# Scan of a hybrid RWKV-7 / Conformer encoder: feature loads on ScalarE's queue, lower blocks and diagonals ahead of the keys at the begin

## The chip, the cores and the metric

The kernel runs on one core of one Trainium2 chip. The metric is the device time of one execution in microseconds; the median of three executions of the kernel before is 2488.1 us (2484.7 to 2490.22).

## The reference

Two groups of tokens (512 and 1024) pass through one encoder layer. What matters here is the RWKV-7 branch: for every head (8 heads of width 64) and for both directions a state is carried over the tokens, and the outputs of the two directions are summed.

```python
def wkv7_scan(r, logw, k, v, a, b, reverse):
    # S_t = S_{t-1} diag(exp(-exp(logw_t))) + (S_{t-1} a_t) b_t^T + v_t k_t^T ;  y_t = S_t r_t
    def step(S, inp):
        r_t, w_t, k_t, v_t, a_t, b_t = inp
        sa = jnp.einsum('bhij,bhj->bhi', S, a_t)
        S = (S * w_t[:, :, None, :] + sa[..., :, None] * b_t[..., None, :]
             + v_t[..., :, None] * k_t[..., None, :])
        return S, jnp.einsum('bhij,bhj->bhi', S, r_t)
    ...
```

Ahead of it lie a norm and one projection into 38 column tiles; after it come a Conformer convolution branch, the merge of the branches, an output projection and a layer of 16 experts of which each takes its best tokens.

## The kernel before, in words

The program has three stages one after the other: `project` and `scan` in one block, then `mixing`, then `experts`. The change lies in the scan and in one helper that `project` uses as well.

**The scan** cuts the 1536 tokens into 24 chunks of 64 (`NCH`), numbered i = 0 to 23 in the order in which a direction d takes them. Within a chunk the recurrence is turned into matrix work: products of the features of a chunk with each other (`products`, `products_c`, lines 376 to 410), masked on VectorE (`masked`, `masked_c`, L412 to L433), a triangular inverse, and then the step itself: `solve` (L1502), `full` (L1516), `state` (L1528). The products run `AHEAD` = 4 chunks ahead of the step. `body(i)` (L1548) is the order of TensorE in step i: `level_n` (L1472) of chunk i, `solve` of chunk i - 1, `level_x` (L1485, L1489), `full(0)` of chunk i - 1, products of chunk i + 4, and so on. `body_first` (L1573) is its order at the begin: the levels of chunk 0, and the products of chunks 2, 3 and 4. L384, L387, L392 and L395 are lines of `products`, and L408 is that of `products_c`.

**Features.** The factors that `products` multiplies are written to HBM by `project` and read back in pairs of chunks. `features(sp, m)` (L345) issues two loads of 1 MB, one for each direction, into one of two buffers (m % 2), after waiting until the products and the receptance copies of pair m - 2 are done. `project` issues m = 0 and 1; the scan issues m = 2 to 11, all of them on SyncE's queue (L1386, L1398, L1433), m = 2 and 3 at the begin and the others in steps 2, 4, ..., 16.

**The triangular inverse.** The lower block of a chunk goes from SBUF to HBM (`lower`, L355, four issues for a chunk), and its 16x16 diagonal blocks come back in another layout (`diagonal`, L363, two issues). For a pair of chunks GpSimd inverts the diagonal blocks (`invert`, L1717), SyncE stores them (`inverses`, L1361) and loads them in the layout of the step (`compact`, L1371), GpSimd spreads them (`expand`, L1739, whose instruction is L1745), and TensorE's `level_n` reads the result.

**SyncE's queue** holds all loads of the scan in an order that is written out by hand (L1383 to L1450): per step also `tokens` (L1330, four issues), `keys` (L1343) and `values` (L1352), two issues each. A wait holds all that stands behind it.

**ScalarE** (L1679 to L1709) in step i: two `gh` copies (`solved`, what `full` reads), the `xx` copies of the levels, the receptance copies of chunk i + 4, and the output copies with their stores to HBM. After step 9 it also computes an inverse root (`conv_root`, L1656), after steps 12 and 13 `conv_silu`.

**VectorE** at the begin (L1913 to L1933): `masked` and `masked_c` of chunks 2, 3 and 4 with the levels of chunk 0 among them, and `started()` (L1788), which writes the decay factors, a state of zeros and identities that step 1 is the first to read. It stands between the work on chunk 3 and that on chunk 4:

```python
            for d in DIRS:
                e.masked_c(dve, d, 3, EARLY)
            started()
            e.masked(dve, 0, AHEAD, EARLY)
            e.masked(dve, 1, AHEAD, EARLY)
```

## Time and profile before

| | |
|---|---|
| median of three executions | 2488.1 us (2484.7 to 2490.22) |
| profiled execution | 2486.42 us, its span 2484.6 us |
| TensorE busy | 2329.5 us (94%) |
| VectorE busy | 1823.7 us (73%) |
| ScalarE busy | 1211.8 us (49%) |
| GpSimd busy | 722.4 us (29%) |
| mean granted TensorE clock | 0.975 |
| SyncE's DMA queue | 412.52 MB in 275552 packets |
| ScalarE's DMA queue | 37.82 MB in 11296 packets |
| queue of instructions (q8) | 1.95 MB in 119 packets |
| feature loads | 24 issues of 1 MB, median 6.1 us from issue to landing |

The span runs from the first to the last instruction of the profiled execution; its own time is 1.8 us longer. Busy time of TensorE is that of matmuls, whose ends are modelled, so a TensorE that is busy is not one at its peak. The scan takes the stretch from about 760 to 1160 us, the projection what lies ahead of it. In the rows, PE is TensorE's matmul, PEld its weight load, DVE VectorE, ACT ScalarE, POOL GpSimd, SPq SyncE's queue; "[3.31 <-DVE all L422]" means that the engine was idle for 3.31 us before the row and that VectorE's instruction of line 422 released it, and "<-issue" that nothing which the profile shows held it.

### The profile page before, as it was taken

How to read it: one execution, taken by the hardware profiler on the slowest of the kernel's cores; microseconds unless marked ns; L12 is line 12 of the kernel's file. 1: busy time of each engine (PE TensorE's matmuls, PEld its weight loads, DVE VectorE, ACT ScalarE, POOL GpSimd, SP SyncE). 2: the span in 40 equal slices, each digit the busy share in tenths (PEclk: the TensorE clock that was granted, in tenths of full speed). 3: DMA queues.
4: the chain of work that ended last, by engine and by line, in shares of the span. 5: the costliest groups of instructions: out<-in, count | busy, mean ns of one | idle time of the engine just before them, and what ended most of it. 6: DMA issues, size and time to landing. Idle time of an engine off the chain costs nothing. (4 is left out here: it accounts for less than half of the span.)

```text
span 2484.6 us, 50105 instructions
## 1 busy us (share of the span) xinstructions
PE 2329.5 (94%) x19520; PEld 2034.6 (82%) x19520; DVE 1823.7 (73%) x2475; ACT 1211.8 (49%) x1751; POOL 722.4 (29%) x721
## 2 busy tenths in 40 slices
PE   6899999999998999987999995799999999999997
PEld 3688888888887999985766674799999999999996
DVE  4547888988895676674767677677777777777777
ACT  5355444544522334433334332665656666666556
POOL 2233243442422444464454535011111111101111
PEclk9999999999998999998999997899999999999998
DMA  4325243352566766763647352877777777777777
GB/s 153 86 88 163 92 158 115 114 174 73 169 206 187 208 190 192 194 169 109 222 128 253 111 198 99 322 256 260 261 246 239 251 259 254 246 252 266 261 254 245
DMA packets 294772, 479.74 MB, mean 193 GB/s; under 512 B 142224, under 2 KB 209952, under 8 KB 266832
## 3 DMA queue, kind: packets, MB, share of 16 engines
q1 hardware_dynamic: 275552, 412.52, 50.5%
q0 software_dynamic: 7760, 27.08, 4.9%
q10 hardware_dynamic: 11296, 37.82, 4.7%
q8 instruction: 119, 1.95, 0.3%
q14 instruction: 45, 0.37, 0.0%
HBM read 363.51 MB, written 110.69 MB: 191 GB/s over the span
## 5 line engine op out<-in xcount | busy, mean ns | idle before, releaser
L2975 PE MATMUL bank<-e_xt,e_w_high 128*128 128x384 f32 x1792 | 525.3, 357 | 3.5 <-DVE e_xt L3143 2.2
L3130 DVE TENSOR_TENSOR e_w_low<-e_w,e_w_high 128x2048 fp32r<-128x2048 f32 x192 | 436.4, 2286 | 69.3 <-ACT e_w_high L3031 69.3
L2976 PE MATMUL bank<-e_xt,e_w_low 128*128 128x192 f32 x1792 | 449.3, 251 | 0.0
L3031 ACT ACTIVATE e_w_high<-e_w 128x2048 fp32r<-128x2048 f32 x192 | 366.5, 1909 | 108.0 <-PE bank L2997 79.3
L2976 PEld LDWEIGHTS bank<-e_xt,e_w_low 128*128 128x128 f32 x1792 | 342.5, 191 | 0.6
L2975 PEld LDWEIGHTS bank<-e_xt,e_w_high 128*128 128x128 f32 x1792 | 338.2, 189 | 5.3 <-issue 2.5
L712 PE MATMUL bank<-h_high,w_high 128*128 128x512 f32 x864 | 259.3, 408 | 1.2 <-DVE work L1158 1.2
L1141 DVE SCALAR_TENSOR_TENSOR work<-work,vec 128x1551 f32<-128x1551 f32 x116 | 243.2, 2096 | 2.2
L715 PE MATMUL bank<-h_low,w_high 128*128 128x512 f32 x864 | 244.2, 391 | 0.0
L718 PE MATMUL bank<-h_high,w_low 128*128 128x512 f32 x864 | 243.5, 390 | 0.0
L2909 POOL DMA_INDIRECT xacc_dram<-e_y,e_put x30 | 47.3, 1577 | 648.3 <-DVE e_y L3165 643.8
L838 POOL TENSOR_TENSOR w_low<-w,w_high 128x1024 fp32r<-128x1024 f32 x38 | 100.4, 2641 | 317.0 <-ACT w_high L887 317.0
L715 PEld LDWEIGHTS bank<-h_low,w_high 128*128 128x128 f32 x864 | 162.6, 188 | 35.6
L718 PEld LDWEIGHTS bank<-h_high,w_low 128*128 128x128 f32 x864 | 162.2, 188 | 34.8
L712 PEld LDWEIGHTS bank<-h_high,w_high 128*128 128x128 f32 x864 | 155.1, 189 | 34.1 <-issue 8.2
L3223 DVE TENSOR_TENSOR e_sums<-bank,e_sums 128x192 f32<-128x192 f32 x256 | 79.2, 350 | 140.1 <-ACT e_sums L3076 140.1
L2144 POOL TENSOR_TENSOR x_w_low<-x_w,x_w_high 128x1024 fp32r<-128x1024 f32 x48 | 118.7, 2473 | 143.2 <-ACT x_w_high L2409 143.1
L3076 ACT ACTIVATE e_sums<-bank 128x192 f32<-128x192 f32 x256 | 70.7, 328 | 150.4 <-PE bank L2979 150.3
L1622 ACT ACTIVATE xx<-bank 128x512 f32<-128x512 f32 (+1 forms) x96 | 46.8, 492 | 171.4 <-PE bank L1485 148.2
L1013 ACT ACTIVATE work<-bank 128x512 f32<-128x512 f32 x84 | 49.9, 594 | 154.3 <-PE bank L741 139.9
L2937 PE MATMUL bank<-e_w_high,e_hid_parts 128*128 128x512 f32 x256 | 103.8, 406 | 0.0
L2939 PE MATMUL bank<-e_w_high,e_hid_parts 128*128 128x512 f32 x256 | 100.1, 391 | 0.0
(385 smaller groups left out, 5119.0 us busy)
## 6 DMA issues: line engine op xcount, KB each, us to landing
e_w<-in_ew SPq DMA_DIRECT2D x192, 1024.0 KB, 5.3
features_dram<-work SPq DMA_DIRECT2D x48, 512.0 KB, 3.3
front<-features_dram SPq DMA_DIRECT2D x24, 1024.0 KB, 6.1
x_w<-in_w_mix SPq DMA_DIRECT2D x48, 512.0 KB, 4.8
w<-in_w_in ACTq DMA_DIRECT2D x35, 512.0 KB, 3.6
ba_tok_dram<-work SPq DMA_DIRECT2D x96, 128.0 KB, 2.4
gates_dram<-work ACTq DMA_DIRECT2D x16, 768.0 KB, 4.6
all<-ba_tok_dram SPq DMA_DIRECT2D x56, 128.0 KB, 3.3
```

The source lines that it names most:

```text
L712: nc.tensor.matmul(bank(t, b)[:], w_high[t % 2][:, c], h_high[:, k, tok(b)], start=(k == 0), stop=False)
L715: nc.tensor.matmul(bank(t, b)[:], w_high[t % 2][:, c], h_low[:, k, tok(b)], start=False, stop=False)
L718: mm = nc.tensor.matmul(bank(t, b)[:], w_low[t % 2][:, c], h_high[:, k, tok(b)], start=False, stop=(k == KD - 1))
L838: tt(w_low[t % 2][:], w[:], w_high[t % 2][:].bitcast(F32), ALU.subtract).then_inc(w_split, 1)
L1141: ch.link(stt(acc, cin[:, tap:tap + n_acc], wt, acc, ALU.mult, ALU.add))
L2144: tt(w_low[s % 2][:], w[s % 2][:], w_high[s % 2][:].bitcast(F32), ALU.subtract).then_inc(w_split, 1)
L2937: nc.tensor.matmul(out, left[0], right[0], start=first, stop=False)
L2939: return nc.tensor.matmul(out, left[1], right[0], start=False, stop=last)
L2975: nc.tensor.matmul(*wide, start=(k == 0), stop=False)
L2976: nc.tensor.matmul(*narrow, start=False, stop=False)
L3031: nc.scalar.activation(w_high[n % RING][:], w[n % RING][:], ACT.Copy).then_inc(w_high_done, 1)
L3130: tt(w_low[n % RING][:], w[n % RING][:], w_high[n % RING][:].bitcast(F32), ALU.subtract)\
```

## The change

`features` takes the engine that issues it. In the scan all its calls move from SyncE's queue to ScalarE's: pair 2 ahead of step 0, pair 3 in step 0 behind the receptance copies of chunk 3, and the pairs of the even steps 2 to 16 at the beginning of the step, ahead of `solved`. At the begin SyncE issues `compact(1)`, then all lower blocks of chunks 2 and 3, then both their diagonals, and only then `keys(0)`, `values(0)`, `tokens(1)`, `keys(1)` and `values(1)`. On VectorE `started()` moves ahead of `masked` of chunk 3.

```diff
--- before.py
+++ after.py
@@ -342,14 +342,14 @@
 
         eng.wait_ge(e.l_f[d][i // 2 % 2], 16 * (i // 4 + 1))
 
-    def features(sp, m):
+    def features(eng, m):
 
         for d in DIRS:
             if m >= 2:
-                sp.wait_ge(e.m_c[d], 2 * m - 2)
-                sp.wait_ge(e.a_r[d], 2 * m - 2)
+                eng.wait_ge(e.m_c[d], 2 * m - 2)
+                eng.wait_ge(e.a_r[d], 2 * m - 2)
             c = m if d == 0 else N_PAIRS - 1 - m
-            sp.dma_start(e.FE[d][m % 2].rearrange("p h x t -> p (h x t)"),
+            eng.dma_start(e.FE[d][m % 2].rearrange("p h x t -> p (h x t)"),
                          g.features[d, c, :, :, :].rearrange("p h c -> p (h c)")).then_inc(e.l_f[d][m % 2], 16)
 
     def lower(sp, d, i):
@@ -1383,19 +1383,18 @@
             tokens(0)
             inverses(0)
             compact(0)
-            e.features(sp, 2)
             compact(1)
-            tokens(1)
-            sp.wait_ge(g.projected, N_TILES)
-            keys(0)
-            values(0)
             for i in (2, 3):
                 for d in DIRS:
                     e.lower(sp, d, i)
-                e.diagonal(sp, i)
+            sp.wait_ge(g.projected, N_TILES)
+            e.diagonal(sp, 2)
+            e.diagonal(sp, 3)
+            keys(0)
+            values(0)
+            tokens(1)
             keys(1)
             values(1)
-            e.features(sp, 3)
 
             def finished(i):
 
@@ -1429,8 +1428,6 @@
                     compact(i + 1)
                 if 1 <= i < NCH - 1:
                     tokens(i + 1)
-                if i % 2 == 0 and 2 <= i < NCH - AHEAD - 2:
-                    e.features(sp, (i + AHEAD + 2) // 2)
                 if i % 2 == 1 and i >= 3 and i + 1 < NCH:
                     compact(i + 1)
                 if i == 1:
@@ -1676,7 +1673,10 @@
                 nc.scalar.activation(small[:, 2, :, :], small[:, 1, :, :], ACT.Sqrt, bias=g.c("eps", 1, 1),
                                      scale=1.0 / HD).then_inc(f_rooted, 1)
 
+            e.features(act, 2)
             for i in range(NCH):
+                if i % 2 == 0 and 2 <= i < NCH - AHEAD - 2:
+                    e.features(act, (i + AHEAD + 2) // 2)
                 if i >= 1:
                     for d in DIRS:
                         solved(d, i - 1)
@@ -1686,6 +1686,8 @@
                     if i == 0:
                         for d in DIRS:
                             receptance(d, 2 + n)
+                if i == 0:
+                    e.features(act, 3)
                 for d in DIRS:
                     if i + AHEAD < NCH:
                         receptance(d, i + AHEAD)
@@ -1915,6 +1917,7 @@
                 level_n(d, 0, 0)
             e.masked(dve, 0, 2, LATE)
             e.masked(dve, 1, 2, EARLY)
+            started()
             e.masked(dve, 0, 3, LATE)
             e.masked(dve, 1, 3, EARLY)
             levels(0, 1)
@@ -1925,7 +1928,6 @@
                 e.masked_c(dve, d, 2, LATE)
             for d in DIRS:
                 e.masked_c(dve, d, 3, EARLY)
-            started()
             e.masked(dve, 0, AHEAD, EARLY)
             e.masked(dve, 1, AHEAD, EARLY)
             for d in DIRS:
```

## Rows read from the trace of the kernel before

**Rows 1.** Windows: length, busy PE PEld DVE ACT POOL, PEclk, DMA share, GB/s.

```profile
759.60:789.60 30.00, 20.11 (x444) 19.10 (x445) 14.99 (x32) 8.40 (x17) 9.47 (x21) 0.84 0.82 227
789.60:1105.00 315.40, 303.00 (x7550) 288.04 (x7549) 215.57 (x386) 124.41 (x243) 143.35 (x355) 0.98 0.70 191
```

**Rows 2.** Timeline of TensorE, begin of the scan: start, duration, line, [idle before <-releaser].

```profile
763.23 0.66 PE L387 MATMUL bank<-front 64*64 64x64 f32 x16
...
768.72 0.21 PE L1485 MATMUL bank<-t,work 64*64 64x64 f32 x1 [2.71 <-issue]
...
779.43 1.09 PE L384 MATMUL bank<-front 64*64 64x128 f32 x16 [0.99 <-DVE py L432]
780.33 0.66 PE L392 MATMUL bank<-front 64*64 64x64 f32 x16
784.30 1.12 PE L387 MATMUL bank<-front 64*64 64x64 f32 x16 [3.31 <-DVE all L422]
...
788.25 1.65 PE L408 MATMUL bank<-front 64*64 64x64 f32 x26 [1.12 <-DVE all L422]
...
791.72 2.93 PE L1502 MATMUL bank<-work,xx 64*64 64x128 f32 x32
...
804.54 1.15 PE L408 MATMUL bank<-front 64*64 64x64 f32 x32
...
807.68 1.92 PE L1502 MATMUL bank<-work,xx 64*64 64x128 f32 x32
```

**Rows 3.** Timeline of VectorE in the same stretch.

```profile
764.80 1.02 DVE L422 TENSOR_TENSOR all<-bank,work 128x256 f32<-128x256 f32 x2 [0.32 <-PE bank L395]
771.80 1.02 DVE L422 TENSOR_TENSOR all<-bank,work 128x512 f32<-128x512 f32 x2 [5.97 <-PE bank L392]
...
779.36 0.65 DVE L1793 TENSOR_TENSOR work<-ends,work 64x96 f32<-64x96 f32 x2
...
783.23 1.02 DVE L422 TENSOR_TENSOR all<-bank,work 128x512 f32<-128x512 f32 x2
...
790.27 1.30 DVE L432 TENSOR_TENSOR py<-bank,work 64x512 f32<-64x512 f32 x2 [2.07 <-PE bank L408]
...
805.74 1.30 DVE L432 TENSOR_TENSOR work<-bank,work 64x512 f32<-64x512 f32 x2 [0.40 <-PE bank L408]
```

**Rows 4.** Windows after the second idle stretch and in the tail of the scan.

```profile
1112.00:1121.00 9.00, 5.97 (x156) 5.34 (x152) 7.30 (x12) 2.51 (x6) 7.53 (x20) 1.00 0.39 99
784.00:786.00 2.00, 1.70 (x24) 1.70 (x26) 0.25 (x1) 0.00 (x0) 1.59 (x5) 0.50 0.69 213
```

**Rows 5.** TensorE's waits in the scan: us in total, times, longest.

```profile
PE bank L1472 <- issue: 4.4, 5, 1.5
...
PE bank L1516 <- ACT gh L1622: 1.5, 2, 1.2
```

**Rows 6.** Timelines of SyncE's queue and of GpSimd at the begin.

```profile
759.90 8.41 SPq L1339 DMA_DIRECT2D work<-ba_tok_dram  x4
...
799.55 2.09 POOL L1745 TENSOR_TENSOR work<-work 128x512 f32<-128x512 f32 x2 [4.09 <-DMA work<-x_dram]
```

**Rows 7.** The issues of `features` (min/median/max ns of one) and their landings.

```profile
L352 SPq DMA_DIRECT2D front<-features_dram x24: 376/477/1648, 706.8 to 1035.4; - x24
...
DMA to landing us min/median/max: 5.1/6.1/9.8
```

**Rows 8.** Timeline of ScalarE, at the begin, in step 2 and before step 10.

```profile
765.73 0.60 ACT L1622 ACTIVATE xx<-bank 128x512 f32<-128x512 f32 x1 [4.64 <-PE bank L1489]
...
808.77 0.60 ACT L1622 ACTIVATE gh<-bank 128x512 f32<-128x512 f32 x1 [1.23 <-PE bank L1502]
...
811.51 0.60 ACT L1622 ACTIVATE xx<-bank 128x512 f32<-128x512 f32 x1 [0.34 <-PE bank L1489]
...
938.73 0.63 ACT L1661 ACTIVATE ya<-ya 128x512 f32<-128x512 f32 x1
```

**Rows 9.** Timeline of TensorE in step 2: `full`, which reads `gh`.

```profile
811.39 1.16 PE L1516 MATMUL bank<-gh,work 64*128 64x128 f32 x16
```

## The prediction

> **What bounds the kernel now.** The windows come first. The change touches the scan alone, and in its steady part, 789.6 to 1105 us, TensorE is busy for 303.0 of 315.4 us at 0.98 of its full clock, while VectorE is busy for 215.6 and ScalarE for 124.4 [rows 1]. What shortens a wait of another engine there brings nothing. The 30 us before it, the begin of the scan, look different: TensorE is busy for 20.1 of 30.0 us, at a mean clock of 0.84 [rows 1]. The timelines of TensorE and VectorE say why [rows 2, 3]. There are two large idle stretches. The first, 2.71 us before 768.72, has "issue" as its releaser: no engine was late, the instructions were. The second, 3.31 us before 784.30, ends on VectorE. TensorE wants `masked(0, 4)`; but VectorE runs `started()` from 779.36 to 783.23, 3.87 us of preparation (decay factors, a zero state, identities) that nothing needs before step 1, and only then `masked(0, 4)`. After that stretch the granted clock is 0.50 [rows 4], the lower of the two levels, 1.2 GHz: sixteen products that follow each other in 0.66 us at 763.23 take 1.12 at 784.30 [rows 2].
>
> The list of TensorE's waits in the scan is the third view: its largest entries are VectorE and "issue" (4.4 us in 5 waits at L1472), one of ScalarE's `gh` copies is there with 1.5, and the loads that this change moves are not in it [rows 5].
>
> **The change, part by part.** I take `started()` first, since it carries the gain, although the title of the change does not speak of it.
>
> *`started()` earlier.* It goes between `masked(1, 2)` and `masked(0, 3)`. There VectorE ends at 764.80 + 1.02 = 765.82 and idles for 5.97 us, to 771.80 [rows 3]. The 3.87 us fit. The first half of `masked(0, 4)` can then start about 0.2 us after the products of L392 end, at 780.33 + 0.66 + 0.20 = 781.19 instead of 783.23 [rows 2, 3]: **2.0 us** earlier, all on TensorE's path. What is late next is this half itself, 1.02 us, so about 1.3 us of idle remains. The cover is the idle of VectorE; were TensorE's "issue" stretch of 2.71 us not there, the same 3.87 us would end about 1 us after the data of `masked(0, 3)`, but everything would also be some 2.7 us earlier (bounds for this term: 0.9 and 2.0).
>
> *The clock behind it.* From that stretch to L1502 at 791.72 the products run at the lower level. If the 3.3 us of idle shrink to 1.3, I expect no fall: the idle stretches followed by one here were 2.71 and 3.31 us long, whereas in the tail TensorE is idle for 3.0 of 9.0 us, in shorter pieces, and the clock stays 1.00 [rows 2, 4]. The saving on the path, each piece at either level: L387 and L395 until VectorE can go on, 788.25 - 1.12 - 784.30 = 2.83 against 764.80 - 763.23 = 1.57, so 1.3; L408 until `masked_c` starts, 790.27 - 788.25 = 2.02 against 805.74 - 804.54 = 1.20, so 0.8; L1502, 2.93 against 1.92, so 1.0 [rows 2, 3]. Together **3.1 us**. Bounds: 0 if the clock falls all the same, 3.1 if it never does; I take 3.1, as the remaining idle pieces are nearer to the tail's than to 2.71.
>
> *Lower blocks and diagonals ahead.* SyncE no longer issues `tokens(1)`, `keys(0)` and `values(0)` before `lower` of chunks 2 and 3 (the third and fourth). The four issues of `tokens(1)` alone took 8.41 us, from 759.90 [rows 6]; the blocks of chunk 3 still wait for `masked(1, 3)`, which VectorE starts only after 771.80 + 1.02. So the last diagonal comes sooner by something between 0 and 8.4 us, an estimate; I take 2, since the mask is the later of the two. `invert(1)` on GpSimd, the compacted inverses and `expand(., 2)` follow it. `expand(., 2)` ends at 799.55 + 2.09 = 801.64 [rows 6]; TensorE reads it some 1 us ahead of L1502 at 807.68 [rows 2], near 806.7. It is off the path by 5 us, and by 2 once TensorE is 5 us earlier. Without this part that margin would be nil: it is cover for the gain, worth **0** by itself (0 to -0.5). The loads passed over are wanted only by and after `full` of step 1, past L1502; they go out at about 779 to 786 and, with landings of a few us, are in time. `compact(1)`, no longer behind 2 MB of features, is early: 0.
>
> *Features off SyncE.* Ten pairs of issues leave, 20 x 0.477 = 9.5 us of SyncE's time [rows 7]. No wait of TensorE ends on what SyncE does behind them [rows 5]: **0**.
>
> *Features on ScalarE.* Each pair costs about 2 x 0.477 = 1.0 us there, and 2 x 1.648 = 3.3 at the slowest pace seen [rows 7]. The four semaphores have been reached: the products were read in the step before, and the copies are ScalarE's own. Queued behind a pair are the two `gh` copies, for `full`, and the `xx` copies, for the second level. Before step 2 ScalarE idles 1.23 us before `gh` [rows 8]; `gh` ends at 809.37 while `full` reads it at 811.39 [rows 8, 9], and the last `xx` copy waits for TensorE, not for ScalarE (0.34 us at 811.51) [rows 8]. A pair of 1.0 us is swallowed by the idle alone: 0. `features(2)` meets 4.64 us of idle before 765.73 [rows 8]; issued near 761.5 behind the gate store, with 9.8 us at the slowest landing [rows 7], it lands near 771, a few us later behind the store, and TensorE reads it first at 779.43 [rows 2]. `features(3)` lies in a long idle of ScalarE. One place has no cover: before step 10 `conv_root` ends at 938.73 + 0.63 = 939.36 [rows 8], and TensorE's `full` already waits 1.2 us for that `gh` [rows 5]. There a pair adds **1.0 us** (0.8 to 3.3).
>
> Sum: -2.0 - 3.1 + 1.0 = -4.1 us. The profiled execution took 2486.4 us, its span 2484.6; it becomes 2482.3. The median of the runs shown, 2488.1, lies 1.7 above it, so I predict 2484.0. About 5 us, 0.2%, is what a measurement of this kernel can tell from no change: the forecast lies just inside.
>
> **Rivals.**
>
> *A: the clock falls anyway* (chance 0.2). For it: 0.99 us of idle before 779.43, then 1.3 before L387 and 1.1 before L408 stand close together [rows 2], and the first fall needed only 2.71 us. Then -2.0 + 1.0 = -1.0: 2487.
>
> *B: ScalarE becomes the bound, slower* (0.08). The place is the pair of issues before `gh` in steps 2, 4 to 16. Cover is 1.23 us of idle plus 811.39 - 809.37 = 2.0 [rows 8, 9]; it decides once a pair takes more than 3.2 us. At the slowest single issue seen a pair takes 3.3; if the four `tokens` issues, 8.41 us behind a features load, are the measure [rows 6], a pair takes 4.2, and each of 8 steps loses 1.0, step 10 another 3.2: about -5.1 + 8 + 4 = +7, 2495. Against: the median issue is 0.477 us.
>
> *C: instruction supply gets worse, slower* (0.07). TensorE's "issue" waits are 2.71 us once and 4.4 at L1472, about 10 us with the smaller ones [rows 2, 5]; the program is unrolled, and the page of the profile lists a DMA queue of its own for instructions, so code comes in while features load. Were those waits to double, -4.1 + 10 = +6: 2494. The Trainium skill, DMA: Bandwidth & Descriptors, section Queues, rings and completion order, says that each DMA engine goes round its queues packet by packet; a second data queue would then leave the code's queue one turn in three instead of one in two while features flow, which speaks for C. No row here shows the order of the turns.
>
> *D: instruction supply gets better* (0.15). The same waits shrink by half, since the loads start earlier in the step, ahead of `solved`, and beside other traffic: -4.1 - 5 = -9, 2479. The Trainium skill, Runtime: NRT & Kernel Launch, section Instruction fetch mechanics, holds that fetching is mostly hidden by the pace of issue; the 2.71 us say otherwise.
>
> *My forecast* keeps 0.5.
>
> **How the numbers follow.** The range reaches from a little past D, 2478, to past A with the slow bound of step 10 added (+2.3), 2490.5; it leaves out B and C and the rest of D's tail. Faster by over 0.2% means under 2483.1: half of the forecast's own spread (0.5 x 0.45) plus D and a little of A, 0.38. Slower: B, C, 0.12 with half of their mild ends counted as same. Within: 0.50.
>
> **What would show it.** Right: the idle before L387 falls from 3.31 to 1.3 us, `started()` stands near 766 to 770, the clock over 784 to 794 is full, TensorE's step 2 starts about 5 us earlier against the end of the projection, `gh` in even steps stays unwaited for, and step 10 shows a wait of 2.2 us for `gh`. Wrong: a clock of 0.50 after 784 (A); waits of L1516 on `gh` in all even steps (B); "issue" waits far from 10 us (C, D); or TensorE waiting for L1745 at step 2, which would say that the diagonals were on the path after all.

## The result, and the profile after

The changed kernel takes 2522.1 us (median of four executions, 2512.0 to 2528.1) against 2489.0 for the kernel before (four executions, 2484.7 to 2490.2), measured together: a ratio of 1.0132, 95% interval 1.0106 to 1.0158. It is 33 us slower, where 4 us less were forecast. Its profiled execution took 2511.97 us, the fastest of the four, so the traces account for the low end of the difference, with a span of 2510.2 us, 25.6 us more than the span of before; the mean granted clock is 0.971 instead of 0.975.

The lines have moved a little: `level_n` is L1469, `level_x` L1482, `solve` L1499, `full` L1513, `state` L1525, the copies of ScalarE L1619, GpSimd's `expand` L1747. On SyncE's queue L360 is `lower`, L373 `diagonal`, L1368 `inverses`, L1380 `compact`, L1358 `values`, in both kernels.

**The begin.** Windows of the kernel after (columns as in [rows 1]), then TensorE's and VectorE's timelines, which answer to [rows 2, 3]:

```profile
759.60:789.60 30.00, 22.98 (x596) 21.70 (x591) 19.18 (x40) 9.34 (x20) 10.20 (x31) 1.00 0.96 256
789.60:1105.00 315.40, 282.18 (x6832) 267.59 (x6834) 187.50 (x339) 114.14 (x224) 121.95 (x292) 0.94 0.64 172
784.00:794.00 10.00, 6.70 (x129) 6.08 (x126) 4.88 (x9) 0.67 (x2) 4.96 (x18) 0.91 0.72 146
```

```profile
756.99 0.68 PE L1469 MATMUL bank<-work 64*64 64x64 f32 x16 [0.70 <-issue]
...
772.54 1.09 PE L384 MATMUL bank<-front 64*64 64x128 f32 x16 [0.85 <-DVE py L432]
775.21 0.68 PE L387 MATMUL bank<-front 64*64 64x64 f32 x16 [1.11 <-DVE all L422]
...
780.54 1.96 PE L1499 MATMUL bank<-work,xx 64*64 64x128 f32 x32 [0.56 <-DVE py L432]
...
790.88 0.56 PE L1469 MATMUL bank<-xx,nl 64*64 64x64 f32 x11 [3.30 <-issue]
...
792.67 1.12 PE L387 MATMUL bank<-front 64*64 64x64 f32 x16
...
799.70 1.15 PE L1469 MATMUL bank<-work 64*64 64x64 f32 x32
...
762.33 0.65 DVE L1795 TENSOR_TENSOR work<-ends,work 64x96 f32<-64x96 f32 x2
...
765.41 0.76 DVE L1800 COPY pre<-work 64x512 f32<-64x512 f32 x2
```

VectorE runs `started()` from 762.33 to 766.2, in the gap that was there for it; the idle before L387 is 1.11 us, and the products behind it run at the full clock (0.68 us for sixteen, where [rows 2] has 1.12). The first 30 us have a clock of 1.00 instead of 0.84. At 790.88 a stretch of 3.30 us with "issue" as its releaser follows, and L387 behind it, at 792.67, takes 1.12 us again. The first row of L1469 stands at 756.99, its counterpart of before, L1472, at 760.40; step 2 begins at 799.70 and began at 806.70 (row below). So the begin takes 42.7 us instead of 46.3: **3.6 us are gained**, where 5.1 were forecast.

That 3.6 is a balance of three parts. From the first `level_n` to the products of L384 (779.43 before [rows 2], 772.54 after) it is 15.6 us instead of 19.0: 3.5 less, in a stretch that `started()` does not touch; the "issue" stretch of 2.71 us that lay there before is gone, one of 1.26 us is left. From L384 to the end of the `solve`, where the forecast put its gain, it is 10.0 us instead of 15.2: 5.3 less. From there to step 2 it is 17.2 us instead of 12.1: 5.2 more, with the new stretch of 3.30 us and slower products behind it.

**The steady part.** In 315.4 us TensorE does 6832 instructions instead of 7550, and its clock is 0.94 instead of 0.98 [rows 1]. The waits of TensorE say what it lacks (us in total, times, longest); first the kernel after:

```profile
PE bank L1469 <- POOL work L1747: 30.4, 10, 14.1
PE bank L1513 <- DVE fu L1823: 11.6, 6, 4.5
...
PE bank L1469 <- issue: 4.3, 3, 3.3
...
PE bank L387 <- DVE all L422: 1.1, 1, 1.1
```

and the same line of the kernel before:

```profile
PE bank L1472 <- POOL work L1745: 1.4, 2, 1.1
```

1.4 us in 2 waits have become 30.4 in 10. All of them are `level_n` of an even step waiting for GpSimd's `expand`; the 10 lie in seven steps, since the two halves of a step can each wait. The entry "issue" at this line, which rivals C and D of the forecast speak of, is unchanged (4.3 against 4.4 us [rows 5]). From the `solve` of step 2 (800.68 after, 807.68 before) to the `state` products behind the last wait for `fu`, one of 1.38 us in both (1184.44 and 1156.71), it is 383.8 us instead of 349.0. Of these 34.7 us the waits on `expand` are 29.0. Other waits in the stretch are about 5 us shorter than before ("issue" 2.0 instead of 5.6, `gh` 0.2 instead of 1.5), and TensorE is busy for 337.0 us instead of 326.2 with the same 8110 products, at a granted clock of 0.94 instead of 0.99. So the lower clock costs about 11 us: behind the longest wait `level_n` takes 2.12 us for its 32 products, and 1.15 without a wait, and `solve` 3.62 us instead of 1.92 (rows below). Ahead of the begin the kernel is 3.4 us earlier, at the begin it gains 3.6, and the rest, -2.1, lies behind the scan: -3.4 - 3.6 + 34.7 - 2.1 = 25.6.

**Where a wait comes from.** The largest is 14.1 us. The timelines of the kernel after around it, one group for each of ScalarE's queue, SyncE's queue, GpSimd and TensorE:

```profile
970.21 0.59 ACT L1619 ACTIVATE work<-bank 64x512 f32<-64x512 f32 x1
...
971.39 1.19 ACTq L352 DMA_DIRECT2D front<-features_dram  x2
988.03 0.60 ACT L1619 ACTIVATE gh<-bank 128x512 f32<-128x512 f32 x1 [17.23 <-PE bank L1499]
...
971.92 1.12 SPq L1380 DMA_DIRECT2D work<-x_dram  x2
...
967.53 0.62 POOL L1739 COPY work<-work 128x256 f32<-128x256 f32 x1
983.06 2.04 POOL L1747 TENSOR_TENSOR work<-work 128x512 f32<-128x512 f32 x2 [14.91 <-DMA work<-x_dram]
...
984.16 2.12 PE L1469 MATMUL bank<-work 64*64 64x64 f32 x32 [14.10 <-POOL work L1747]
986.07 3.62 PE L1499 MATMUL bank<-work,xx 64*64 64x128 f32 x32
```

ScalarE is done with the last copies of step 11 at 970.80, comes to the head of step 12 and issues 2 MB of features at once, 17 us ahead of the `gh` copies that stand behind them in its program. Half a microsecond later SyncE issues the `compact` load of 64 KB for which step 12 itself is waiting. It lands 11.0 us later. The list of transfers (KB each, median us to landing) issued in 968 to 984 us, of the kernel after; then the same `compact` load of the kernel before, issued at 957.82, 15 us ahead of that step's features:

```profile
front<-features_dram ACTq DMA_DIRECT2D x2, 1024.0 KB, 9.2
...
work<-x_dram SPq DMA_DIRECT2D x2, 64.0 KB, 11.0
```

```profile
work<-x_dram SPq DMA_DIRECT2D x2, 64.0 KB, 3.6
```

11.0 us and 3.6 us for the same load. A second way leads over SyncE's queue. Step 2 shows its beginning, and step 4 the first large wait (timelines of the kernel after, ScalarE's queue, SyncE's queue, TensorE):

```profile
801.12 1.06 ACTq L352 DMA_DIRECT2D front<-features_dram  x2
...
801.08 3.01 SPq L360 DMA_DIRECT2D g_dram<-work  x4
804.13 1.35 SPq L1358 DMA_DIRECT2D st<-v_tok_dram  x2
810.81 0.86 SPq L373 DMA_DIRECT2D work<-g_dram  x2
...
833.86 2.12 PE L1469 MATMUL bank<-work 64*64 64x64 f32 x32 [3.73 <-POOL work L1747]
```

The features go out together with the four `lower` issues of chunk 5. `diagonal` may go once these blocks have landed in HBM; it goes at 810.81, 5.3 us after `values` is through; in the kernel before the same one went at 809.88, 0.1 us after `values`, from `lower` issues at 805.08, though elsewhere it also waits there, for up to 3.8 us. The inversion, `inverses`, `compact` and `expand` of that pair follow it, and 23 us later TensorE waits 3.73 us.

This first wait, however, is not the price of the moved loads. The inversion of that pair begins at 813.60 in the kernel after and at 813.71 in the kernel before, so it is not later; TensorE is earlier. With these loads back at their old place (e1 below) the wait in step 4 is 4.43 us. The price of the delay shows in the rounds behind it: GpSimd's idle time before the `expand` of the odd step, which waits for the `compact` loads behind `diagonal`, is 11.80, 11.42, 12.22 and 12.24 us in steps 4 to 10 (at 846.60, 881.04, 917.73 and 951.98), where the kernel before has 8.53, 6.65, 8.30 and 6.58 us at 845.55, 875.68, 909.13 and 940.14.

Two of the small transfers of the chain in the steady part, `diagonal` (L373) and `compact` (L1380) (min/median/max of issue in ns; us from issue to landing), 790 to 1110 us, first of the kernel after, then of the kernel before:

```profile
L373 SPq DMA_DIRECT2D work<-g_dram x38: 326/489/1399, 794.1 to 1106.8; - x38
...
DMA to landing us min/median/max: 1.8/2.8/10.8
L1380 SPq DMA_DIRECT2D work<-x_dram x36: 377/508/2835, 792.3 to 1093.3; - x36
...
DMA to landing us min/median/max: 2.1/3.4/11.1
```

```profile
L373 SPq DMA_DIRECT2D work<-g_dram x40: 324/482/2366, 798.5 to 1097.9; - x40
...
DMA to landing us min/median/max: 1.8/2.9/4.9
L1380 SPq DMA_DIRECT2D work<-x_dram x40: 377/506/1751, 797.5 to 1099.7; - x40
...
DMA to landing us min/median/max: 2.0/2.8/4.5
```

The medians hardly move; the longest go from 4.9 to 10.8 us and from 4.5 to 11.1 us. With the margin of the next paragraph, one late load in a round is enough.

**The margin that was not looked at.** Why do a few microseconds on GpSimd's side reach TensorE at all? GpSimd is busy for 29% of the span. But its work for a pair of chunks is a chain, one round for two steps. A round in the kernel before, GpSimd, and TensorE's `level_n` of two even steps (in a timeline the two halves of `expand`, about 1.0 us each, are one row):

```profile
867.00 2.04 POOL L1745 TENSOR_TENSOR work<-work 128x512 f32<-128x512 f32 x2 [7.75 <-DMA work<-x_dram]
875.68 2.11 POOL L1745 TENSOR_TENSOR x<-work 128x512 f32<-128x512 f32 x2 [6.65 <-DMA work<-x_dram]
877.75 0.73 POOL L1730 TENSOR_TENSOR work<-work 128x256 f32<-128x256 f32 x1
...
889.52 0.97 POOL L1737 COPY work<-work 128x256 f32<-128x256 f32 x1
898.79 2.04 POOL L1745 TENSOR_TENSOR work<-work 128x512 f32<-128x512 f32 x2 [8.30 <-DMA work<-x_dram]
...
869.73 1.15 PE L1472 MATMUL bank<-work 64*64 64x64 f32 x32
...
901.64 1.15 PE L1472 MATMUL bank<-work 64*64 64x64 f32 x32
```

`expand` for the even step ends at 869.04, TensorE starts at 869.73: 0.7 us. The next ends at 900.83, TensorE starts at 901.64: 0.8 us. The same difference is 1.7 us at 838.67, 0.5 at 934.04, 2.3 at 965.99. TensorE reads the second half about 0.6 us into its row, so the true margin is 1 to 3 us. The `expand` of the odd step (875.68) starts the inversion (877.75 to 890.49), then come a store and a load, and `expand` again: 25.2 us of 31.9 for two steps, and the rest goes on the lower blocks and diagonals that SyncE waits for. GpSimd has 71% of the span idle and here no more than 1 to 3 us to give.

### The profile page after: what moved, and what is told of

It is laid out like the page before. It is cut to its first block and busy times, and to the rows that moved or that the text cites. A ratio compares the mean times of both kernels' runs of the same rounds, so it can differ in the third digit from the quotient of the medians.

```text
span 2510.2 us, 50106 instructions
## 1 busy us (share of the span) xinstructions
PE 2338.2 (93%) x19520; PEld 2042.3 (81%) x19520; DVE 1819.5 (72%) x2475; ACT 1211.4 (48%) x1751; POOL 721.3 (29%) x721
## 5 line engine op out<-in xcount | busy, mean ns | idle before, releaser
L1619 ACT ACTIVATE xx<-bank 128x512 f32<-128x512 f32 (+1 forms) x96 | 46.9, 491 | 172.6 <-PE bank L1482 150.9
```

## The experiments

In all of them "expand wait" is TensorE's wait in the `level_n` of even steps on GpSimd in the one profiled execution. It differs between kernels by a few us without meaning: e10 below, as fast as the kernel before, has 6.4 us where that has 1.4. Times and ratios are to the kernel before on the same chip; e1 to e4, e5 to e8, e9 to e12 and e13 to e16 shared a chip each. Costs that were measured in different groups, the kernel after among them, are compared by their ratios with their intervals.

**1. Which part of the change costs.** Two kernels cut the change in two: `e1_steady_back` is the kernel after with the features of steps 2 to 16 again on SyncE, `e2_steady_only` the kernel before with these loads alone moved.

```diff
@@ e1_steady_back, against the kernel after @@
             for i in range(NCH):
-                if i % 2 == 0 and 2 <= i < NCH - AHEAD - 2:
-                    e.features(act, (i + AHEAD + 2) // 2)
...
+                if i % 2 == 0 and 2 <= i < NCH - AHEAD - 2:
+                    e.features(sp, (i + AHEAD + 2) // 2)
                 if i % 2 == 1 and i >= 3 and i + 1 < NCH:
                     compact(i + 1)
```

> The changed kernel, but the feature loads of steps 2 to 16 are back on SyncE's queue at their old place, behind `tokens`. What stays of the change is the begin: `started()` earlier, lower blocks and diagonals ahead, pairs 2 and 3 on ScalarE. Theory T (the 2 MB of a pair are under way at the head of an even step, when the lower blocks of the step before go out and the diagonals and inverses come back; that chain is what GpSimd's inversion waits for, and its `expand` then keeps TensorE waiting): the loss goes and the gain of the begin stays, 3 to 7 us below the kernel before, and no wait of TensorE on `expand` over 2 us. Rival W (the new order at the begin sets the chain late): it stays about 30 us above. Rival I (the issues take ScalarE's time): as T, so this run does not tell T from I.

> The kernel before with one thing changed: the feature loads of steps 2 to 16 are issued on ScalarE's queue at the head of the step. Begin and VectorE as before. T and I: 30 to 40 us above the kernel before, since the gain of the begin is missing. W: within 5 us of the kernel before.

e1: 2487.4 against 2484.9 us, 1.0014 [0.9999, 1.003]. e2: 2527.7 us, 1.0181 [1.0161, 1.0202]. The loss is all in the steady loads; alone they cost even more, 43 us, above the 30 to 40 expected, with an expand wait of 39.9 us. In e2 the `compact` load for step 4 goes out at 834.91, 1.7 us behind the pair, GpSimd begins on it only at 845.62, and TensorE waits 14.78 us: what step 12 of the kernel after shows, without any change of the begin. That e1 gains nothing from the better begin was not expected. Its list of TensorE's waits has two entries that grew, and its timeline shows where the larger wait is:

```profile
PE bank L1471 <- issue: 9.7, 7, 3.6
...
PE bank L1471 <- POOL work L1747: 6.2, 3, 4.4
```

```profile
837.43 2.31 PE L1471 MATMUL bank<-work 64*64 64x64 f32 x32 [4.43 <-POOL work L1747]
```

The wait of 4.4 us stands in step 4, at the chain's next deadline behind step 2: TensorE comes sooner and GpSimd does not. The "issue" waits at this line are 5.3 us more than the 4.4 of the kernel before; both entries together are larger than the gain of the begin, and e1 does not tell their shares apart.

**2. The transfer or its place.** `e3_small_loads` is the kernel after whose loads from the fifth pair on (m = 4) fetch only 128 of the 2048 columns, from the same place in the same number of issues; its products of later chunks therefore use features that are not theirs. `e4_between_levels` issues the full loads on ScalarE between the copies of the first and the second level. `e5_head_on_sync` issues them on SyncE, but at the head of the step, as the kernel after does.

```diff
@@ e3_small_loads @@
     def features(eng, m):
+        n = HP * 8 * CH if m < 4 else 2 * CH
...
-            eng.dma_start(e.FE[d][m % 2].rearrange("p h x t -> p (h x t)"),
-                         g.features[d, c, :, :, :].rearrange("p h c -> p (h c)")).then_inc(e.l_f[d][m % 2], 16)
+            eng.dma_start(e.FE[d][m % 2].rearrange("p h x t -> p (h x t)")[:, 0:n],
+                         g.features[d, c, :, :, :].rearrange("p h c -> p (h c)")[:, 0:n]).then_inc(e.l_f[d][m % 2], 16)
@@ e5_head_on_sync, the two lines taken from ScalarE @@
+                if i % 2 == 0 and 2 <= i < NCH - AHEAD - 2:
+                    e.features(sp, (i + AHEAD + 2) // 2)
                 if 1 <= i and i + AHEAD - 1 < NCH:
                     e.diagonal(sp, i + AHEAD - 1)
```

> The changed kernel with the same issues and waits at the same places, but from pair 4 on a load brings only the first 128 of 2048 columns, 64 KB instead of 1 MB (the products of the later chunks are then made from stale features). T: the waits of TensorE on `expand` go, 3 to 8 us below the kernel before. I: the issues are all there, so the loss stays, 20 to 30 us above.

> The changed kernel with the steady feature loads still on ScalarE's queue, but issued between the copies of the first and the second level, some 4 to 5 us later in the step. T in its plain form (what counts is when the transfer runs): the lower blocks have landed by then and the diagonals are out, so most of the loss goes, at most 8 us above the kernel before. T2 (what counts is that the loads are on a second queue, which is served beside SyncE's small transfers instead of in order with them): 15 to 30 us above.

> The changed kernel, with the feature loads of steps 2 to 16 at the same point of the step, its head, but on SyncE's queue, ahead of the diagonal. There they stand behind the compact loads for the same step, which were issued one step before, and ahead of the diagonal and of the compact loads for the next step. T2 (a second queue is what lets 2 MB run into small loads already issued): most of the loss goes, 0 to 10 us above the kernel before. T (what counts is that 2 MB run at the head of an even step, on whatever queue): the diagonals and the compact loads behind them are as late as in the changed kernel, 15 to 35 us above.

e3: 2479.3 us, 0.9972 [0.996, 0.9983], expand wait 7.8 us, none over 3.6. With the issues in place and the bytes gone, the loss is gone; what ScalarE spends on issuing is not it. e4: 2495.4 us, 1.0033 [1.0016, 1.0049], expand wait 13.6 us: most of the loss is gone, though at 10 us above it stands just outside the 8 expected. e5: 2512.4 against 2488.1 us, 1.0093 [1.0062, 1.0124], expand wait 34.4 us in 16 waits. So without any load on ScalarE's queue in the steady part the place at the head costs 24 us.

e5 is not the same moment as the kernel after, though: from step 4 on SyncE issues the pair 2 to 4 us behind the begin of `level_n` (842.82 against 839.90, 914.14 against 912.29), where ScalarE in the kernel after issues up to 12.8 us ahead of it (971.39 against 984.16). The cleaner comparison of the queues is e7 of the next group of runs, on the same chip as e5, where ScalarE issues at nearly e5's moment, 3 to 5.5 us behind the begin of `level_n` (878.70 against 875.69, 918.72 against 913.23). It measures 2510.6 us, 1.0087, and e5 2512.4, 1.0093: no difference between the queues that is clear of noise. The Trainium skill, DMA: Bandwidth & Descriptors, section Issuing engines are not separate DMA queues, says that transfers of all issuing engines run on the same 16 DMA engines and interleave, and that a second issuing engine saves only the time of the issue. This case agrees with the consequence of the first (e5 and e7 cost the same) and with the second (issues alone cost nothing, e3); which engines carried a load no run shows.

**3. The moment on ScalarE.** `e7_behind_gh` puts the pair behind the `gh` copies, which wait for TensorE's `solve`; a step that is late can then no longer issue ahead of its own `compact`. `e8_behind_levels` puts it behind the second level's copies.

```diff
@@ e7_behind_gh @@
                         solved(d, i - 1)
+                if i % 2 == 0 and 2 <= i < NCH - AHEAD - 2:
+                    e.features(act, (i + AHEAD + 2) // 2)
                 for n in range(LEVELS):
@@ e8_behind_levels @@
                 if i == 0:
                     e.features(act, 3)
+                if i % 2 == 0 and 2 <= i < NCH - AHEAD - 2:
+                    e.features(act, (i + AHEAD + 2) // 2)
```

> The changed kernel, with the steady feature loads on ScalarE's queue but behind the two `gh` copies of the step. ScalarE can then issue them only after TensorE has begun the step, so they can no longer run into the compact loads that the same step waits for; they still run into the diagonal and into the compact loads for the next step. If the feedback (a late step, whose compact loads are still on their way, is met by the features issued meanwhile) makes most of the loss: 5 to 12 us above the kernel before. If the collision with the next step's loads makes most of it: 20 us or more above.

> The changed kernel, with the steady feature loads on ScalarE's queue behind the copies of the second level, ahead of the receptance copies, about 12 us into the even step. GpSimd is in the middle of its inversion then and no load of the inverse chain is under way. T: no loss is left, 0 to 6 us below the kernel before, at least as fast as with the loads back on SyncE. T2 in its strong form (any features load on the second queue costs): 10 us or more above.

e7: 2510.6 us, 1.0087 [1.0057, 1.0118]; 5 expand waits, none over 7.6 us where the kernel after had one of 14.1, but 30.8 us in total, as much as its 30.4. e8: 2492.9 us, 1.0029 [1.0012, 1.0046], expand wait 11.0 us in 13 waits. So e7 came out as expected for the collision with the next step's loads (20 us or more), not for the feedback (5 to 12). The pair ahead of the `gh` copies may be worth 11 of the 33 us, but the intervals of e7 and of the kernel after overlap, and the total of the waits does not show it. The rest of the cost falls as the pair goes out later: it is issued 3 to 5.5 us behind the begin of `level_n` in e7, 5 to 8 in e4, and 12 to 15 in e8, at 1.0087, 1.0033 and 1.0029 (the kernel before issues it 7 to 9.4 us behind, on SyncE). e8 stays 5 us above the kernel before where it was expected below. Its SyncE timeline shows one place of it:

```profile
881.82 3.60 SPq L360 DMA_DIRECT2D g_dram<-work  x4
885.47 1.68 SPq L1358 DMA_DIRECT2D st<-v_tok_dram  x2
893.29 0.95 SPq L373 DMA_DIRECT2D work<-g_dram  x2
894.28 0.49 SPq L1368 DMA_DIRECT2D x_dram<-work  x1
```

The features of this step were issued on ScalarE at 882.26, beside the `lower` issues at 881.82; `diagonal` goes 6.1 us after `values` is through, and `inverses` stands behind it.

**4. The begin alone, and a change of order on SyncE.** `e6_started_only` is the kernel before with `started()` moved. Four kernels put `compact(i + 1)` of an even step ahead of its `diagonal`, so that it cannot be held by the lower blocks: e9 from e1, e10 from the kernel before, e11 from e8, e12 from the kernel after.

```diff
@@ e9_swap_steady_back, e10, e11, e12 @@
+                if i % 2 == 0 and i >= 4:
+                    compact(i + 1)
                 if 1 <= i and i + AHEAD - 1 < NCH:
                     e.diagonal(sp, i + AHEAD - 1)
                 if i % 2 == 1 and 3 <= i < NCH - 3:
                     inverses((i + 1) // 2)
-                if i % 2 == 0 and i >= 4:
-                    compact(i + 1)
```

> The kernel before with `started()` alone moved ahead of the masks of chunk 3. The prediction's term: 5.1 us less by step 2, the clock included. If the inverse chain has its own time, that gain is given back at step 4, where TensorE then waits for `expand`: 0 to 3 us below the kernel before at the end. If it is kept: 4 to 6 us below.

> e1 (new begin, steady feature loads on SyncE) with one more swap on SyncE's queue: in even steps from 4 the compact loads for the next step go ahead of the diagonal, which waits for the lower blocks to land. Theory: the inverse chain (expand, inversion, store, compact loads, expand) takes as long as two steps of TensorE, so what shortens it lets the gain of the begin be kept. The swap takes the wait for the lower blocks, 1 to 3 us, out of each round of the chain: 3 to 7 us below the kernel before, no wait of TensorE on `expand` over 1 us from step 6 on. If the chain is not the bound: as e1, within 4 us of the kernel before.

> The kernel before with the swap alone. There TensorE hardly waits for `expand`, so a shorter chain has nothing to give: within 3 us of the kernel before, on either side. GpSimd's `expand` of the odd chunks starts 1 to 3 us earlier after TensorE's step.

> e8 (all of the change, steady feature loads on ScalarE behind the second level's copies) with the same swap. Theory: 2 to 7 us below the kernel before, that is 6 us or more below e8. If not the chain but the loads on ScalarE as such keep e8 slow: as e8, 5 to 8 us above.

> The changed kernel with the same swap. The 2 MB still run at the head of the even step, beside the compact loads for this step and ahead of those for the next, but the wait for the lower blocks no longer adds to them: 10 to 25 us above the kernel before. If the slow landing of the lower blocks alone carried the loss: under 5 us above.

e6: 2487.8 against 2488.1 us, 1.0003 [0.9988, 1.0018]. From L384 to the end of the `solve` it takes 10.0 us (778.54 to 788.49), so the 5.3 us of the move are there in full. TensorE then waits for `expand` in steps 2 and 4, by 1.38 and 2.45 us, and the `solve` behind the first wait takes 3.31 us instead of 1.92: the chain takes most of the gain back. "issue" waits are some 4 us more than before as well, and their part is not known. e9: 2485.2 against 2487.5 us, 0.9981 [0.9966, 0.9995]; a part of the gain now stays, 2 of the 3 to 7 us expected, though its expand wait in one execution, 5.2 us, is not clearly below e1's 6.2. e10: 2490.5 against 2487.5 us, 1.0003 [0.9985, 1.002]; its expand wait of 6.4 us has one of 4.6 in step 4. e11: 2492.5 us, 1.0022 [1.0008, 1.0036], no better than e8. e12: 2514.7 us, 1.0097 [1.0066, 1.0127], with one execution profiled at 2523.9 and this list of waits:

```profile
PE bank L1469 <- POOL work L1747: 43.2, 5, 15.1
```

By the ratios the order on SyncE would be worth about 9 us of 33 there, but the intervals of e12 and of the kernel after overlap, so that it gives anything is not shown. Waits of up to 15.1 us stay, so the slow landing of the lower blocks alone does not carry the loss.

**5. A late chain by itself.** `e13_longer_inversion` adds no transfer. It puts four more copies on GpSimd into each inversion of the kernel before, about 2.6 us a round.

```diff
+                for _ in range(4):
+                    ch.link(nc.gpsimd.tensor_copy(XB[s][r, :, 0, :], x.rearrange("p r c -> p c r")))
                 nc.gpsimd.tensor_copy(XB[s][r, :, 0, :], x.rearrange("p r c -> p c r")).then_inc(p_c, 1)
```

> The kernel before with four more copies of 128x256 on GpSimd in every inversion, about 0.65 us each, 2.6 us more in each of the 10 full rounds of the inverse chain (and in two half ones at the end), and nothing else: no load, no queue is touched. Theory (the chain has 0.5 to 3 us of slack in two steps of TensorE): a good half of the 26 us shows, 10 to 25 us above the kernel before, with TensorE waiting on `expand` in even steps. If the slack were over 3 us a round, the loss of the change would need something besides a late chain: under 5 us above.

2508.5 against 2487.1 us, 1.0076 [1.0052, 1.0101]: about 20 us, where some ten rounds of 2.6 us would be 26 and the margins take up the first of each. Its waits:

```profile
PE bank L1472 <- POOL work L1747: 13.5, 9, 3.8
...
PE bank L1472 <- POOL x L1747: 3.7, 1, 3.7
```

Nothing but GpSimd's round was made longer, and most of it appears in the time. This run shows that a late chain costs that much by itself, with no transfer moved. That the chain is also what carries the loss of the kernel after is read from its waits, of which only the entry for `expand` grew by more than 1 us.

**6. Toward a better version.** `e14_split_pairs` is e9 with the two loads of a pair taken apart: direction 0 in the even step, direction 1 in the odd step behind `compact`, both on SyncE. `e15_inverses_first` (from e8) and `e16_inverses_first_back` (from e9) put `inverses` ahead of `diagonal` in odd steps.

```diff
@@ e14_split_pairs, against e9 @@
                 if i % 2 == 0 and 2 <= i < NCH - AHEAD - 2:
-                    e.features(sp, (i + AHEAD + 2) // 2)
+                    e.features(sp, (i + AHEAD + 2) // 2, (0,))
                 if i % 2 == 1 and i >= 3 and i + 1 < NCH:
                     compact(i + 1)
+                if i % 2 == 1 and 3 <= i < NCH - AHEAD - 1:
+                    e.features(sp, (i + AHEAD + 1) // 2, (1,))
```

> e9 (new begin, steady feature loads on SyncE, compact loads ahead of the diagonal) with every pair of feature loads taken apart: the load of one direction in the even step at the old place, that of the other in the odd step behind its compact loads. Bursts of 1 MB instead of 2. Theory: less for the lower blocks and keys to wait behind, so 0 to 4 us below e9, that is 4 to 8 us below the kernel before.

> e8 (all of the change, steady feature loads on ScalarE behind the second level's copies) with the store of the inverses ahead of the diagonal in odd steps. In e8 the lower blocks landed behind the features after up to 12.7 us, and the diagonal that waits for them held the finished inverses behind it on SyncE's queue. Theory: that wait is what is left of the loss in e8, so 3 us above to 4 below the kernel before. If sharing the DMA engines at large keeps e8 slow: 5 us or more above.

> e9 with the same order, the store of the inverses ahead of the diagonal in odd steps. There the lower blocks land in time as a rule, so it gives 0 to 3 us over e9: 2 to 7 us below the kernel before.

e14: 2482.0 against 2487.1 us, 0.998 [0.9965, 0.9995], the lowest of the kernels that compute everything, 5 us below the kernel before and about 40 below the changed one (each against its own measurement of the kernel before: 0.998 and 1.0132). Its expand wait is 5.4 us in its profiled execution, which was the slowest of twelve, 2493.7 us; what lowers its time the trace does not show. The load in the odd step goes out 3 to 10 us ahead of the next even step there, and no cost of that 1 MB is seen. e15: 2493.0 us, 1.0019 [1.0005, 1.0033]. e16: 2486.0 us, 0.9988 [0.9972, 1.0004], expand wait 3.5 us. e9, e14 and e16 cannot be told from each other: their intervals overlap. e15 misses as e11 did: what holds e8 up by 5 us is neither the order of `compact` nor that of `inverses`. It shows as many small waits (13 of at most 4.3 us in e8, 13 of at most 2.9 in e15) and stays open. Both runs came out in the branch of their expectations that blames the loads on ScalarE as such, or the sharing of the DMA engines (5 us or more above). That 2 MB beside the lower blocks make some landing late in most rounds would fit too, and no run tells these apart.

## Why the prediction was wrong

**The step that failed** is the term "Features off SyncE", put at 0 on the ground that "No wait of TensorE ends on what SyncE does behind them", together with "Features on ScalarE", where a pair was priced as two issues against the idle time ahead of `gh`. The issues cost nothing, as forecast (median 0.54 us, e3). What was left out is that moving an issue moves 2 MB of traffic. In the kernel before, the pair went out behind `diagonal`, `compact` and `tokens` of its step, when the `compact` loads had as a rule landed (in step 6 `expand` begins on them at 875.68, and the pair goes at 878.38). At the head of the step it goes out with them. Measured price: 33 us for the whole change, 43 for these loads alone (e2), 24 for about the head of the step on SyncE (e5), nothing without the bytes (e3).

**The reading that let it through.** The list of waits before shows GpSimd with 1.4 us, and a wait that is absent was taken for a margin that is wide. The forecast looked at one margin, that of step 2 (5 us), for its own gain. The ends of `expand` set beside the starts of `level_n` would have shown 1 to 3 us in the even steps from 4 to 12. A chain of two steps' length that ends just in time is a second bound.

**A feedback** was not seen either, and how much it costs stays open. ScalarE's issue at the head of a step waits for nothing of that step, so the later TensorE is, the further ahead of the step the pair goes, among the loads that the step itself waits for: 17 us ahead of `gh` at 971.39. With the pair behind `gh` (e7) the longest wait falls from 14.1 to 7.6 us, but the total of the waits stays, and the 11 us by which the cost is lower are not clear of the intervals.

**`started()` earlier and the clock behind it** went as written: the place on VectorE, 1.1 us of idle instead of 3.31, the full clock in L387, 1.96 us instead of 2.93 for the `solve` at 780.54. The two terms, 2.0 and 3.1 us, measure 5.3 together between L384 and the end of the `solve`, in the kernel after and in e6. That 3.6 us arrived at step 2, near the forecast, is partly luck: 3.5 us came from a stretch ahead that the forecast left alone, and 5.2 went again behind the `solve`, with an "issue" wait of 3.30 us after which the clock fell. "the clock over 784 to 794 is full" was wrong for this reason (0.91). The error lay in carrying the gain to the end: e6, which has this part alone, measures 1.0003. With a second bound 1 to 3 us behind, 5 us less on TensorE's side cannot be worth 5.

**Lower blocks and diagonals ahead** was called cover for step 2, and in the kernel after TensorE did not wait there (1.15 us at 799.70, no wait). e6 shows that without them it does, by 1.38 us, as the forecast had it. But the cover is thin: of the thirteen kernels profiled with the new begin, seven wait for `expand` in step 2 all the same, e9 by 4.22 us and e7 by 5.09. e2, without the begin's changes, is 10 us slower than the whole change is; part of that may be these earlier diagonals, but it was not tried alone.

**Step 10** was to cost 1.0 us in a `gh` wait of 2.2. It did not: the entry for `gh` fell from 1.5 to 0.2 us, but TensorE is itself late there. In e3, with the issues at the same place and little waiting, the wait in step 10 is 0.82 us, against 1.24 before, so the term is nothing there too.

**The rivals.** B named the right sign and the wrong mechanism: no pair took 3.2 us to issue, and `gh` is hardly waited for. C and D fall by their numbers: "issue" waits at `level_n` are 4.3 us, and all of them in the scan about 8 where 10 stood. Their ground, that such waits hang on which loads are under way, has something for it at the begin (see the last section of this document); that they are fetches of instructions, as the forecast reads the 2.71 us, no run shows. A falls in its form, the clock did not fall at L387. None of them had a load delayed by another transfer, although the forecast quoted 8.41 us for four small issues behind a features load [rows 6].

## What to carry to other kernels

When a large transfer is moved, ask which small loads are under way at the new moment and who waits for them; the queue it is issued from is secondary. For every engine that feeds the bound one, subtract the end of its result from the start of the reader, in several steps: where the difference is small against the landing of a load, the chain is a second bound, however idle its engine is and however short the list of waits. In this kernel a background load is best behind the step's small loads (e4 and e8 against e5 and e7), and behind an instruction that waits for the bound engine; that a late step otherwise makes itself later is seen in one trace and not priced.

## What was unexpected in the hardware

- A load of 64 KB that takes 2.8 us in the median took 11.0 us behind 2 MB issued half a microsecond earlier on the other queue, longer than each of the two loads of 1 MB (9.2 us). The median over all such loads rose only to 3.4 us.
- Waits with the releaser "issue" change from kernel to kernel: at `level_n` 4.4 us before, 4.3 after, 9.7 in e1, 7.0 in e9. They blur differences of 5 us. At the begin they follow the order of the loads, which is not TensorE's own: the five kernels with the old order (before, e2, e6, e10, e13) have one of 2.1 to 2.8 us at `level_x`, near 764 to 769, and none near 791; all thirteen with the new order lack it and have one of 1.7 to 3.7 us between 788 and 795, in the second `level_n` of step 1. Moving `started()` alone (e6) leaves the first in place. No run shows what TensorE waits for there.
- Behind waits of 3.7 to 14 us in the kernel after, `level_n` took 2.12 us instead of 1.15, the lower clock level; behind one of 1.41 us it stayed at 0.68 us for sixteen products, the upper one. In e3, behind 3.56 us, the first half still took 0.68 us and the second 1.12. A long wait on this engine costs more than its length, here about 11 us on top of 29, from the busy time of the same 8110 products.
